# A rebuilt router: logits on unscaled features, a fixed block per expert, token lists by one-hot products

## The chip, the core and the metric

One core of a Trainium2 chip runs one program. The metric is the device time in microseconds (us) of one execution, lower being better; the kernel before is shown by the median of three runs, 2042.06 us (2040.55 to 2044.55). Its profiled execution took 2040.88 us, with a span of 2039.4 us from the first instruction to the last. Times in the tables below are us from the start of the span.

## The reference, cut to what matters

512 tokens of 1024 features pass two layers, an mLSTM and Fourier mixer, and then a mixture of 16 experts in 4 groups. Only its router is changed:

```python
x = x + gate1 * rmsnorm(y, g_post_mix)
h2 = modulate(rmsnorm(x, g_pre_ffn), shift2, scale2)      # h * (1 + scale) + shift
g_logits = h @ w_router_group + b_router_group            # 4 groups
p_group = softmax(g_logits); g_sel = argmax(g_logits)
e_sel = (h @ w_router_expert + b_router_expert)[group g_sel]   # 4 experts
top_v, top_i = top_k(e_sel, 2)
w_top = softmax(top_v) * p_sel
for e in range(16):
    a = silu(h @ w_gate[e]) * (h @ w_up[e])
    y = y + combine[..., e] * (a @ w_down[e])
```

Everything is float32. A token thus goes to two experts; 512 tokens make 1024 pairs.

## The kernel before, in words

Features lie on the partitions, as 8 chunks of 128, and tokens along the columns. Large products are exact to float32 by three passes over high and low parts of the operands (`three_pass`); small ones are plain float32 products on PE. The order on each engine is the order in which the program is written, and every engine waits on counters of the others: `need` adds waits, `do` issues and counts, `join()` makes all engines wait for all. A plain float32 product shows as two rows of the trace, one per pass; a transpose as one.

The projection `w_out_2` (`mix_out`) is streamed by `stream` and `rows_products`: PE multiplies 8 rows of weights into 8 banks, and before its chunk 5 of the first row it runs the last head's transposes (`last_head`, `skip_and_gate`). `rows_root` then forms the root of the mean square, and `Residual.plain` adds the scaled product to X: `chunks` takes the 8 chunks in turn (DVE scales and adds, ACT squares, PE sums the squares over features by four products with a column of ones), `root` takes the root for each token, and `spread` turns it into a row over the columns.

The router (lines 1975 to 2143) then runs step by step:
- 8 multiplications on DVE and 8 additions of the shift on ACT write H2, then `join()`;
- PE forms the logits (32 products and 4 for the bias) and transposes H2 by tokens (32); the 2048 KB of token rows go to HBM (`h2_tokens`);
- DVE chooses a group and two experts by `first_max`, with two visits to ACT for exponentials; PE counts the pairs (`asum`), DVE turns counts into slots. Slots are packed: an expert with n tokens takes ceil(n/128) blocks, one without takes none, and `etab_u` lists the expert of each block;
- POOL scatters the token numbers into a list in HBM (8 indirect DMAs, L2141) and reads the list back (`slot_tokens`);
- `gather(0)` (L2185) fetches the token rows of block 0, `turn_rows` transposes them, `split_rows` splits them.

Weights of a block are 12 units of 512 KB (4 gate, 4 up, 4 down); `fetch` (L2217) issues one on SP's queue, `split_unit` splits one (ACT the high part, DVE the low). The first four of block 0 wait for the table of experts, units 4 and 5 for the scatter, and the others for the first gather. In `block` (L2270) SP fetches the next block's unit as soon as this block's copy is split, PE runs gate, up and down products, and POOL gathers the next block's rows. After the last block, the outputs are gathered by pair and summed.

## Time and profile before

| | us |
|---|---|
| median of three runs | 2042.06 |
| profiled execution | 2040.88 |
| its span | 2039.4 |
| PE busy (share of the span) | 1816.0 (89%) |
| DVE busy | 1217.6 (60%) |
| ACT busy | 917.2 (45%) |
| POOL busy | 112.2 (5%) |

Busy time is summed over the span, and the share hides that the stages differ: the page's 40 slices show PE at 8 or 9 tenths in most, and at 6 in the two from 1580 to 1682 us, which hold most of the router. The granted clock of PE is given as a share of 2.4 GHz: 1.00, or 0.50 for 1.2 GHz. An instruction's row names its output and inputs; "idle before" is how long its engine waited, and for what.

### The profile page before, as it was taken

Reading aid. Unit: us, or ns where it says so; the run is one execution under the profiler, and the core shown is the slowest. Engines: PE = TensorE matmul, PEld = TensorE weight load, DVE = VectorE, ACT = ScalarE, POOL = GpSimd, SP = SyncE. Lnnn points to the kernel's source line nnn. Section 1 sums busy time; section 2 is a strip of 40 time slices with the busy share of each in tenths; the row PEclk is TensorE's granted clock in tenths of the full one; section 3 lists DMA queues with packets and bytes.
Section 4 is the critical chain, followed back from the end, with each engine's and each line's share of the span. In section 5 each row is a group of like instructions: output and inputs, shape, how many; then the busy total and the mean of one; then the engine's idle time right before and its main releaser. Section 6 shows DMA issues by size and latency. Waiting matters only on the chain. (4 is left out here: it accounts for less than half of the span.)

```text
span 2039.4 us, 25515 instructions
## 1 busy us (share of the span) xinstructions
PE 1816.0 (89%) x9142; PEld 1506.0 (74%) x9142; DVE 1217.6 (60%) x2157; ACT 917.2 (45%) x1449; POOL 112.2 (5%) x132
## 2 busy tenths in 40 slices
PE   7897899999998977899999998899877669999993
PEld 6776788888886755778888887785766658888872
DVE  3555668885226556368766324645744358888885
ACT  3446432222224337242223223423833158898984
POOL 1000000000000000001100000100000011011001
PEclk8998899999998989999999997999987679999997
DMA  4323234545322240227544323300120189999993
GB/s 143 90 76 111 72 93 135 145 135 145 103 94 61 64 172 26 76 69 196 165 145 125 102 94 109 85 21 33 53 73 11 47 307 375 372 356 365 353 348 143
DMA packets 206339, 289.88 MB, mean 142 GB/s; under 512 B 14704, under 2 KB 152920, under 8 KB 206120
## 3 DMA queue, kind: packets, MB, share of 16 engines
q1 hardware_dynamic: 188356, 237.98, 35.5%
q0 software_dynamic: 12080, 36.42, 5.8%
q10 hardware_dynamic: 5812, 14.25, 1.9%
q8 instruction: 59, 0.97, 0.2%
q14 instruction: 32, 0.26, 0.0%
HBM read 271.78 MB, written 22.07 MB: 144 GB/s over the span
## 5 line engine op out<-in xcount | busy, mean ns | idle before, releaser
L227 DVE TENSOR_TENSOR weights_low<-ring,weights_high 128x1024 fp32r<-128x1024 f32 x202 | 246.7, 1223 | 407.4 <-ACT weights_high L221 407.3
L200 PE MATMUL bank<-XH,weights_high 128*128 128x512 f32 x1120 | 454.3, 406 | 30.0 <-DVE XL L69 20.3
L202 PE MATMUL bank<-XH,weights_low 128*128 128x512 f32 x1120 | 444.6, 397 | 0.0
L201 PE MATMUL bank<-XL,weights_high 128*128 128x512 f32 x1120 | 443.5, 396 | 0.0
L221 ACT CAST weights_high<-ring 128x1024 fp32r<-128x1024 f32 x202 | 211.1, 1047 | 439.1 <-PE bank L202 438.8
L200 PEld LDWEIGHTS bank<-XH,weights_high 128*128 128x128 f32 x1120 | 215.6, 193 | 78.7 <-ACT squares L69 12.3
L202 PEld LDWEIGHTS bank<-XH,weights_low 128*128 128x128 f32 x1120 | 214.8, 192 | 47.0
L201 PEld LDWEIGHTS bank<-XL,weights_high 128*128 128x128 f32 x1120 | 215.6, 193 | 43.0 <-issue 0.5
L2241 DVE TENSOR_TENSOR XL<-ring,XH 128x1024 fp32r<-128x1024 f32 x144 | 171.2, 1220 | 30.4 <-ACT XH L2235 30.4
L2235 ACT CAST XH<-ring 128x1024 fp32r<-128x1024 f32 x144 | 145.5, 1048 | 0.5 <-PE bank L202 0.3
L69 DVE SCALAR_TENSOR_TENSOR squares<-ring,c_silu,squares 128x128 f32<-128x128 f32 x384 | 135.2, 352 | 13.6
L200 PE MATMUL bank<-hidden_high,weights_high 128*128 128x512 f32 x352 | 137.1, 390 | 0.0
L202 PE MATMUL bank<-hidden_high,weights_low 128*128 128x512 f32 x352 | 137.0, 389 | 0.0
L201 PE MATMUL bank<-hidden_low,weights_high 128*128 128x512 f32 x352 | 136.9, 389 | 0.0
L2241 DVE TENSOR_TENSOR weights_low<-ring,weights_high 128x1024 fp32r<-128x1024 f32 x72 | 86.1, 1218 | 0.1
L189 POOL DMA_DIRECT2D ring<-in_w_ada x48 | 42.4, 884 | 719.9 <-DVE squares L263 719.9
L1111 ACT ACTIVATE tmp<-tmp 128x512 f32<-128x512 f32 x44 | 27.8, 633 | 110.1 <-DVE tmp L1107 110.1
L200 PE MATMUL bank<-weights_high,gathered_high 128*128 128x256 f32 (+1 forms) x216 | 71.4, 331 | 6.2 <-DVE weights_low L2241 5.2
L201 PEld LDWEIGHTS bank<-hidden_low,weights_high 128*128 128x128 f32 x352 | 66.1, 188 | 13.7
L202 PEld LDWEIGHTS bank<-hidden_high,weights_low 128*128 128x128 f32 x352 | 66.1, 188 | 13.7
L200 PEld LDWEIGHTS bank<-hidden_high,weights_high 128*128 128x128 f32 x352 | 66.1, 188 | 13.6
L2235 ACT CAST weights_high<-ring 128x1024 fp32r<-128x1024 f32 x72 | 74.1, 1054 | 0.0
(449 smaller groups left out, 3126.5 us busy)
## 6 DMA issues: line engine op xcount, KB each, us to landing
ring<-in_w_ffn_in SPq DMA_DIRECT2D x88, 512.0 KB, 4.8
ring<-in_w_gate SPq DMA_DIRECT2D x72, 512.0 KB, 5.1
ring<-in_w_up SPq DMA_DIRECT2D x72, 512.0 KB, 7.1
ring<-in_w_down SPq DMA_DIRECT2D x72, 512.0 KB, 5.6
ring<-in_w_ada POOLq DMA_DIRECT2D x48, 512.0 KB, 4.7
ring<-in_w_ffn_out SPq DMA_DIRECT2D x44, 512.0 KB, 3.5
ring<-in_w_out SPq DMA_DIRECT2D x24, 512.0 KB, 3.5
slot_output<-expert_out SPq DMA_DIRECT2D x19, 512.0 KB, 6.7
```

Source lines behind the costliest of these rows:

```text
L69: op(*args, **kw).then_inc(self.line.sem, 1)
L189: queue.eng.dma_start(dst, src).then_inc(ln.sem, 16)
L200: PE.matmul(out_ap, w_h, x_h, start=first, stop=False, skip_group_check=True)
L201: PE.matmul(out_ap, w_h, x_l, start=False, stop=False, skip_group_check=True)
L202: return PE.matmul(out_ap, w_l, x_h, start=False, stop=last, skip_group_check=True)
L221: S.copy(wh[:, s, :], ring[s][:, :]).then_inc(high_done.sem, 1)
L227: V.tensor_tensor(wl[:, s, :], ring[s][:, :], wh[:, s, :].bitcast(F32), ALU.subtract).then_inc(split_done.sem, 1)
L1111: S.activation(sg, sg, ACT.Silu).then_inc(silu_done.sem, 1)
L2235: S.copy(high[s], raw[q]).then_inc(l_high.sem, 1)
L2241: V.tensor_tensor(low[s], raw[q], high[s].bitcast(F32), ALU.subtract).then_inc(l_split.sem, 1)
```

## The change

1. `Residual` gets a router. For each chunk ACT also writes X times the gain (`xg`, unnormalized), and PE multiplies it with the router's weights into bank 1, behind the sums of squares. The root for each token is applied to the logits (`lgm`) and to the token rows (`half_rows`) afterwards; `spread` and H2 are gone. The share of the shift and the bias (`router_row`), the shift as a row (`shift_row`) and a row of column numbers (`iota_row`) are made by 18 products on PE and four copies on ACT ahead of `mix_out`; the router's weights are loaded by POOL's queue before that.
2. Each expert owns block e; only tokens beyond 128 go to further blocks from 16 on. The first 16 entries of the table are constants, and block 0 is expert 0's.
3. Both experts are chosen in all groups at once, the arithmetic of the pair weights comes after `split_rows(0)`, and the exponentials with it.
4. The list of tokens for all blocks comes from eight products of one-hot matrices (`at_place`, `tokens_at`) straight into `idx`; scatter, list in HBM and its load are gone.
5. Eight of block 0's weight units are fetched before the residual chunks, the last four once the token rows are stored, whose tiles they share (`h2t = raw[8:]`). The first four are split before the first gather has landed.

```diff
-                scaled, summed, low, squared = {}, {}, {}, {}
+                scaled, summed, low, squared, routed = {}, {}, {}, {}, {}
...
                     summed[j] = tok
+                    if self.router:
+                        gain, xg, w_router = self.router
+                        pe.need(*bank_free[1], routed[j])
+                        for t in range(TT):
+                            self.logits = pe.do(PE.matmul, bank[1][:, t * 20:(t + 1) * 20],
+                                                xg[:, order[j], t * P:(t + 1) * P], w_router[:, order[j], :],
+                                                start=j + t == 0, stop=False, skip_group_check=True)
...
                     squared[j] = act.do(S.activation, squares[j % 3], X[:, k, :], ACT.Square,
                                         after=[*x_ready[k], *([summed[j - 3]] if j >= 3 else [])])
+                    if self.router:
+                        gain, xg, w_router = self.router
+                        routed[j] = act.do(S.activation, xg[:, k, :], X[:, k, :], ACT.Copy, scale=gain[:, k:k + 1])
...
                 self.root()
-                self.spread()
-                return self.token_root
+                return self.rooted
...
+        load(pool, lr, wrt[:, :, 0:4], I["w_router_group_2"][0].rearrange("(k p) n -> p k n", p=P))
...
+        shift_row = con[:, where["rope_cos"][0]:where["rope_cos"][0] + D]
+        for half in range(2):
+            pe.need(*bank_free[6 + half])
+            for c in range(4):
+                k = 4 * half + c
+                t = pe.do(PE.matmul, bank[6 + half][:, c * P:(c + 1) * P], section(0, SHIFT2)[:, k:k + 1].broadcast_to([P, P]),
+                          ident, start=True, stop=True)
+            shift_ready = act.do(S.copy, shift_row[:, half * 512:(half + 1) * 512], bank[6 + half][:, :],
+                                 after=[t, row_read[6]])
+            bank_free[6 + half] = [shift_ready]
+        pe.need(lr.now(), *bank_free[3])
+        for k in range(KC):
+            pe.do(PE.matmul, bank[3][:, 0:20], section(0, SHIFT2)[:, k:k + 1].broadcast_to([P, P]), wrt[:, k, :],
+                  start=k == 0, stop=False)
+        pe.do(PE.matmul, bank[3][:, 0:20], ones[0:1, :], brow[:, :], start=False, stop=True)
+        t = pe.do(PE.matmul, bank[3][:, P:2 * P], const("token")[:, 0:1].broadcast_to([P, P]), ident, start=True, stop=True)
+        act.do(S.copy, router_row[:, :], bank[3][:, 0:20], after=[t])
+        router_consts = act.do(S.copy, iota_row[:, :], bank[3][:, P:2 * P])
+        bank_free[3] = [router_consts]
         spread = mix_out(I["w_out_2"][0], None, out_order, out_ready, between=last_head)
         m_ctx.close()
-        router_norm = Residual(POST_MIX, spread).plain()
...
-        for k in range(KC):
-            t = vec.do(V.scalar_tensor_tensor, H2[:, k, :], X[:, k, :], PRE_FFN[:, k:k + 1], rstd_t[:, :], ALU.mult,
-                       ALU.mult, after=[router_norm])
-            act.do(S.activation, H2[:, k, :], H2[:, k, :], ACT.Identity, bias=section(0, SHIFT2)[:, k:k + 1], after=[t])
-        join()
-        for t4 in range(TT):
-            for k in range(KC):
-                t = pe.do(PE.matmul, bank[0][:, t4 * 20:t4 * 20 + 20], H2[:, k, t4 * P:(t4 + 1) * P], wrt[:, k, :],
-                          start=k == 0, stop=False, after=[lr.now()])
-            logits = pe.do(PE.matmul, bank[0][:, t4 * 20:t4 * 20 + 20], ones[0:1, :], brow[:, :], start=False, stop=True)
...
-        load(act, lh2, h2d.rearrange("(t p) d -> p t d", p=P), h2t[:, :, :], after=[vec.line.now(), act.line.now()])
...
+        h2t = raw[8:]
...
+        sp.need(split_done.now(), lfill.now())
+        for q in range(UNITS - 4):
+            if q == len(ring):
+                sp.need(vec.line.now(), act.line.now(), pe.line.now(), used_done.now())
+            fetch(0, 0, q, first=True)
+        for q in (act, vec):
+            q.need(vec.line.now(), act.line.now(), pe.line.now(), used_done.now())
+        xg = x_tok[:, :, :].rearrange("p t d -> p (t d)").rearrange("p (k t) -> p k t", k=KC)
+        norm3 = Residual(POST_MIX, spread, router=(PRE_FFN, xg, wrt))
+        token_root = norm3.plain()
+        rstd_c = roots[:, 1, :].unsqueeze(2)
+        def half_turn(i):
+            b = (3, 4, 5, 6, 7, 0)[i % 6]
+            pe.need(*bank_free[b])
...
+                k = 4 * (i % 2) + c
+                t = pe.do(PE.transpose, bank[b][:, c * P:(c + 1) * P], xg[:, k, (i // 2) * P:(i // 2 + 1) * P], ident)
+            half_turned[i] = t
+        def half_rows(i):
+            b, cols = (3, 4, 5, 6, 7, 0)[i % 6], slice((i % 2) * 512, (i % 2 + 1) * 512)
+            t = vec.do(V.scalar_tensor_tensor, h2t[i // 2][:, cols], bank[b][:, :], roots[:, 1, i // 2:i // 2 + 1],
+                       shift_row[:, cols], ALU.mult, ALU.add, after=[half_turned[i], token_root, shift_ready])
+            bank_free[b] = [t]
+            if i % 2:
+                load(sp, lh2, h2d[(i // 2) * P:(i // 2 + 1) * P, :], h2t[i // 2], after=[t])
+        half_turned = {}
+        for i in range(6):
+            half_turn(i)
...
+        vec.do(V.tensor_copy, etab_u[:, 0:NE], iota[:, 0:NE])
+        t = vec.do(V.tensor_tensor, lgm[:, :, :], bank[1][:, 0:TT * 20].rearrange("p (t n) -> p t n", t=TT),
+                   bc(rstd_c, TT, 20), ALU.mult, after=[norm3.logits, token_root, router_consts])
...
+        tm1 = vec.do(V.tensor_reduce, m1[:, :, 0], el[:, :, :], AX, ALU.max, after=[te])
...
+        te = vec.do(V.tensor_tensor, less1[:, :, :], el[:, :, :], bc(m1[:, :, :], TT * 4, 4), ALU.is_lt, after=[tm1])
...
+        te = vec.do(V.scalar_tensor_tensor, less1[:, :, :], less1[:, :, :], 100.0, iota4e, ALU.mult, ALU.add, after=[te])
...
+        te = vec.do(V.tensor_reduce, at1[:, :, 0], less1[:, :, :], AX, ALU.min, after=[te])
...
+        t1 = vec.do(V.tensor_tensor, oh1[:, :, :], iota4e, bc(at1[:, :, :], TT * 4, 4), ALU.is_equal, after=[te])
...
+        t = vec.do(V.tensor_tensor, asum[:, :, :], A[:, 0], A[:, 1], ALU.add, after=[ta, t2])
...
+        pe.need(t, *bank_free[2])
+        ranks, count = bank[2][:, 0:TT * NE], bank[2][:, TT * NE:(TT + 1) * NE]
+        pe.do(PE.matmul, ranks, const("before"), asum[:, :, :].rearrange("p t n -> p (t n)"), start=True, stop=False,
+              skip_group_check=True)
+        for u in range(TT - 1):
+            for v in range(u + 1, TT):
+                t = pe.do(PE.matmul, bank[2][:, v * NE:(v + 1) * NE], ones[:, :], asum[:, u, :], start=False,
+                          stop=u == TT - 2, skip_group_check=True)
+        for u in range(TT):
+            counted = pe.do(PE.matmul, count, ones[:, :], asum[:, u, :], start=u == 0, stop=u == TT - 1,
+                            skip_group_check=True)
+        for i in range(3):
+            half_rows(i)
+        half_turn(6)
+        half_turn(7)
...
+        tr = vec.do(V.tensor_scalar, full1[:, :, :], rank, float(P), None, ALU.is_ge, after=[counted])
...
+        tr2 = vec.do(V.scalar_tensor_tensor, full[:, :, :], rank, float(2 * P), full1[:, :, :], ALU.is_ge, ALU.add, after=[tr])
...
+        tp = vec.do(V.scalar_tensor_tensor, place[:, :, :], full[:, :, :], float(-P), rank, ALU.mult, ALU.add, after=[tr2])
...
+        tc = vec.do(V.tensor_tensor, full1[:, :, :], full1[:, :, :], moved[:, :].unsqueeze(1).broadcast_to([P, TT, NE]),
...
+        tb = vec.do(V.tensor_reduce, blk_j[:, :], a_blk[:, :, :, :].rearrange("p j t n -> p (j t) n"), AX, ALU.add, after=[tb])
+        t = vec.do(V.tensor_tensor, tokens_at[:, :, :], iota[:, 0:BLOCKS].unsqueeze(1).broadcast_to([P, 2 * TT, BLOCKS]),
+                   blk_j[:, :].unsqueeze(2).broadcast_to([P, 2 * TT, BLOCKS]), ALU.is_equal, after=[tb])
...
+        tn = vec.do(V.tensor_tensor, tokens_at[:, :, :].rearrange("p (j t) b -> p j t b", j=2),
+                    tokens_at[:, :, :].rearrange("p (j t) b -> p j t b", j=2),
+                    token_less[:, :].unsqueeze(1).unsqueeze(3).broadcast_to([P, 2, TT, BLOCKS]), ALU.mult, after=[t, tl])
...
+        for i in range(2 * TT):
+            t = vec.do(V.tensor_scalar, at_place[:, i, :], iota_row[:, :], place_j[:, i:i + 1], None, ALU.is_equal)
+            listed = pe.do(PE.matmul, bank[1][:, 0:BLOCKS], at_place[:, i, :], tokens_at[:, i, :], start=i == 0,
+                           stop=i == 2 * TT - 1, after=[t, tn])
+        half_rows(3)
+        half_rows(4)
+        idx_ready = vec.do(V.tensor_scalar, idx[:, :], bank[1][:, 0:BLOCKS], float(T), None, ALU.add, after=[listed])
+        bank_free[1] = [idx_ready]
+        for i in range(5, 8):
+            half_rows(i)
+        cleared = vec.do(V.memset, hg[:, :], 0.0)
...
+        table = vec.do(V.tensor_scalar, etab_u[:, BLOCKS:BLOCKS + 1], inc[:, NE - 1:NE], float(NE - 1), None, ALU.add)
+        empty = vec.do(V.memset, yt[:, :], 0.0)
+        for q in (act, vec):
+            q.need(used_done.now(), split_done.now())
+        for q in range(AHEAD):
+            split_unit(0, q, first=True)
...
+        for q in (pe, act):
+            q.need(*[x for b in range(8) for x in bank_free[b]])
...
+        token_rows()
+        pool.need(idx_ready, cleared, lh2.now())
+        gather(0)
         for q in engines:
             q.need(*[x for b in range(8) for x in bank_free[b]])
-        sp.need(vec.do(V.memset, yt[:, :], 0.0))
-        pool.need(vec.do(V.memset, hg[:, :], 0.0))
...
-        load(pool, l_idx, idx[:, :], idxd.rearrange("(p b) o -> p (b o)", p=P))
-        pool.need(l_idx.now())
-        gather(0)
         turn_rows(0)
         for half in range(2):
             split_rows(0, half)
-        SP.wait_ge(vec.line.sem, table[1])
-        sp.need(lfill.now())
-        e = SP.value_load(etab_u[0:1, 0:1], min_val=0, max_val=NE - 1)
-        for q in range(UNITS):
-            if q == len(ring):
-                sp.need(lh2.now(), vec.line.now(), act.line.now(), pe.line.now(), lsc.now())
-            if q == len(ring) + 2:
-                sp.need((l_hg, 16))
-            fetch(0, e, q, first=True)
-        for q in range(AHEAD):
-            split_unit(0, q, first=True)
+        t = vec.do(V.tensor_tensor, e4[:, :, :], gl[:, :, :], bc(gm[:, :, :], TT, 4), ALU.subtract, after=[tgm])
+        exp1 = act.do(S.activation, e4[:, :, :], e4[:, :, :], ACT.Exp, after=[t])
...
+        t2 = vec.do(V.tensor_reduce, p2[:, :, 0], picked2[:, :, :], AX, ALU.add, after=[t2])
...
+        t = vec.do(V.tensor_tensor, wts[:, 0, :], p1[:, :, 0], psel[:, :, 0], ALU.mult, after=[t, t2])
+        vec.do(V.tensor_tensor, wts[:, 1, :], wts[:, 0, :], p2[:, :, 0], ALU.mult, after=[t])
...
+        r_ctx.close()
+        sp.need(empty, table, lh2.now())
+        for q in range(UNITS - 4, UNITS):
+            fetch(0, 0, q, first=True)
```

On PE, in the chunks of the last residual sum (`xg` is called x_tokens, since it lies in that tile), "-" is before and "+" the change:

```order
-L69 MATMUL bank<-ones,squares 128x1 x8
+L69 MATMUL bank<-ones,squares 128x1 x4
+L69 MATMUL bank<-w_router,x_tokens 128x20 x4
+L69 MATMUL bank<-ones,squares 128x1 x4
+L69 MATMUL bank<-w_router,x_tokens 128x20 x4
 L69 MATMUL bank<-ones,spare 128x1 x4
```

Each group of four sums of squares is now followed by four router products.

On PE, just ahead of the first products of the projection `w_out_2`, after the transposes of the third head:

```order
 L69 MATMUL bank<-state,tmp 128x129
 L69 MATMUL bank<-const_tables,z_and_u 128x128 x4
+L69 MATMUL bank<-const_tables,modulation_biased 128x128 x8
+L69 MATMUL bank<-w_router,modulation_biased 128x20 x8
+L69 MATMUL bank<-b_router,ones 128x20
+L69 MATMUL bank<-const_tables 128x128
 L200 MATMUL bank<-XH,weights_high 128x512
 L201 MATMUL bank<-XL,weights_high 128x512
```

Eighteen small products have come in; nothing has left.

On SP's queue, the last eight units of block 0 before (behind the load of block 0's expert from the table and the four gate units; the names in brackets are counters; slots_scattered counts the scatter, rows_gathered the gather):

```order
L2227 DMA ring<-in_w_up 128x1024 [waits pe_done,act_done,slots_scattered,vec_done,h2_stored]
L2227 DMA ring<-in_w_up 128x1024
L2227 DMA ring<-in_w_up 128x1024 [waits rows_gathered]
L2227 DMA ring<-in_w_up 128x1024
L2227 DMA ring<-in_w_down 128x1024 x4
```

and with the change, from the projection's weights to the loop over blocks:

```order
L189 DMA ring<-in_w_out 128x1024 [waits split_done] x7
L2116 DMA ring<-in_w_gate 128x1024 [waits slot_output_filled,split_done]
L2116 DMA ring<-in_w_gate 128x1024 x3
L2116 DMA ring<-in_w_up 128x1024 [waits pe_done,used_done,act_done,vec_done]
L2116 DMA ring<-in_w_up 128x1024 x3
L189 DMA h_tokens<-ring 128x1024 [waits vec_done] x4
L2116 DMA ring<-in_w_down 128x1024 [waits h2_stored,vec_done]
L2116 DMA ring<-in_w_down 128x1024 x3
```

The waits on the table, the scatter and the gather are gone; the token rows are stored from this queue in four pieces, and only the last four units wait for that.

## Rows read from the trace of the kernel before

**Rows 1.** Windows: the stages; us, busy of PE, PEld, DVE, ACT, POOL, clock, DMA, GB/s

```profile
1550.00:1552.00 2.00, 1.02 (x8) 0.97 (x8) 0.50 (x2) 0.26 (x1) 0.00 (x0) 1.00 0.00 0
1554.64:1571.26 16.62, 13.78 (x64) 13.73 (x64) 11.10 (x17) 5.31 (x10) 0.00 (x0) 0.50 0.00 0
1571.26:1603.25 31.99, 23.32 (x112) 22.50 (x112) 8.13 (x13) 7.94 (x13) 0.00 (x0) 0.55 0.04 3
1603.25:1610.65 7.40, 0.00 (x0) 0.00 (x0) 5.52 (x30) 1.70 (x3) 0.00 (x0) 0.75 0.72 285
1610.65:1616.92 6.27, 6.27 (x29) 6.27 (x30) 0.00 (x1) 0.00 (x0) 0.00 (x0) 0.50 0.01 3
1616.92:1626.13 9.21, 7.17 (x48) 6.93 (x47) 7.40 (x35) 5.19 (x10) 0.00 (x0) 0.80 0.00 0
1626.13:1638.36 12.23, 0.00 (x0) 0.00 (x0) 1.54 (x2) 0.00 (x0) 7.78 (x9) 0.56 0.52 172
1638.36:1652.68 14.32, 1.98 (x8) 1.58 (x8) 2.57 (x4) 3.33 (x5) 3.05 (x5) 0.50 0.57 196
1652.68:1673.89 21.21, 21.17 (x108) 17.89 (x108) 16.87 (x19) 17.63 (x22) 2.10 (x2) 0.87 1.01 387
1673.89:1693.36 19.47, 18.74 (x108) 16.00 (x109) 16.52 (x19) 17.41 (x23) 2.10 (x2) 1.00 0.98 366
```

**Rows 2.** The page's DMA issues: queue, count, KB each, us to landing

```profile
ring<-in_w_gate SPq DMA_DIRECT2D x72, 512.0 KB, 5.1
...
slot_output<-expert_out SPq DMA_DIRECT2D x19, 512.0 KB, 6.7
```

**Rows 3.** Timeline of PE: start, us, instruction, count, idle before and what ended it

```profile
1504.15 1.11 PE L69 MATMUL bank<-const_tables,z_and_u 128*128 128x128 f32 x4 [5.10 <-DVE z_and_u L69]
...
1550.50 1.02 PE L69 MATMUL bank<-ones,tmp 128*128 128x1 f32 x8 [2.84 <-DVE tmp L69]
...
1556.97 3.54 PE L69 MATMUL bank<-ones,squares 128*128 128x1 f32 x16 [2.94 <-DVE tmp L69]
...
1581.21 3.58 PE L69 MATMUL bank<-w_router,h 128*128 128x20 f32 x16 [7.76 <-ACT h L69]
...
1597.48 5.01 PE L69 MATMUL bank<-const_tables,h 128*128 128x128 f32 x32
```

**Rows 4.** Timeline of DVE in the residual sum and the router

```profile
1554.68 0.75 DVE L69 SCALAR_TENSOR_TENSOR tmp<-bank,gains,rstd 128x512 f32<-128x512 f32 x1 [2.65 <-ACT rstd L69]
...
1603.73 0.17 DVE L69 TENSOR_TENSOR r_penalty<-r_logits,r_m 128x16 f32<-128x16 f32 x1
1603.94 0.17 DVE L69 SCALAR_TENSOR_TENSOR r_penalty<-r_penalty,const_tables 128x16 f32<-128x16 f32 x1
...
1610.11 0.23 DVE L69 TENSOR_TENSOR r_pair<-r_group,r_second 128x64 f32<-128x64 f32 x1
1610.37 0.23 DVE L69 TENSOR_TENSOR r_pairs<-r_pair 128x64 f32<-128x64 f32 x1
...
1623.05 0.54 DVE L69 TENSOR_TENSOR r_compare<-r_blocks_to,const_tables 128x368 f32<-128x368 f32 x1
```

**Rows 5.** Timelines of SP, POOL, PE and DVE around the first gather

```profile
1638.21 9.91 SPq L2227 DMA_DIRECT2D ring<-in_w_up  x4
...
1642.03 0.18 POOL L2189 COPY tokens_now<-slot_tokens 128x1 uint32<-128x1 uint32 x1 [3.08 <-DMA slot_tokens<-slot_token]
1643.12 1.07 POOL L2192 DMA_INDIRECT gathered<-h_tokens,tokens_now  x1 [0.91 <-POOL tokens_now L2189]
...
1647.34 1.98 PE L2201 MATMUL bank<-const_tables,gathered 128*128 128x128 f32 x8 [23.24 <-DMA gathered<-h_tokens,tokens_now]
...
1649.97 1.29 DVE L2210 TENSOR_TENSOR gathered_low<-bank,gathered_high 128x512 fp32r<-128x512 f32 x2 [22.14 <-ACT gathered_high L2208]
```

**Rows 6.** DMAs that read h2_tokens (the gathers), and the store that writes it

```profile
DMA to landing us min/median/max: 4.2/6.5/7.5
...
h_tokens<-h_tok ACTq DMA_DIRECT2D x1, 2048.0 KB, 7.0
```

254 lines of the change are left out of this document (113 added, 141 removed).

## The prediction

> **What bounds the kernel now.** I read the page first: the span is 2039.4 us, the profiled execution 2040.88, the median of the runs 2042.06. Then I cut the time around the router into stages, from the moment at 1554.64 when DVE begins the residual sum until the first product of the first expert block at 1652.68. The reader should see in [rows 1] that these seven stages, 98.04 us in all, are one chain that is handed from engine to engine: for most of it one engine works at a time, and what stands behind it can begin only then. From 1652.68 the blocks run, 21.21 us for the first and 19.47 for the next, with PE at 18.74 of 19.47. The DMA share is near 1 there too, but at 387 GB/s in the first block against 366 in the second, so the weights could come faster; PE and its hand-overs set the cadence. So each us that the first product comes earlier is a us off the end, and what follows the blocks is not touched.
>
> The number of blocks must be the same for that. 72 loads of gate weights, 4 per block, make 18 blocks, and 19 output stores fit (one more than blocks) [rows 2]. The new table has 16 blocks plus one for each further 128 tokens of an expert. Worked out from the reference on its inputs, the experts get 20 to 175 tokens, none gets none, and two get over 128 (175 and 138): 18 blocks, as before.
>
> **The change, part by part.** "Gain" is against the profiled execution.
>
> Products beside the chunks. The name promises cover, but in that stage PE is the slow engine: 13.78 of 16.62 us busy from 1556.97 on, while DVE has 11.10 and ACT 5.31 [rows 1, 3]. The sums of squares are 32 float32 products with one column each, and 8 of them take 3.54 us at the clock of 0.50 (1.2 GHz). The router's 32 products have 20 columns and take 3.58 for 8, since it is the 128x128 operand that costs [rows 3]. They go in line: 13.78 + 4 x 3.58 = 28.1, so the logits are there at 1585.0 and the stage lasts 30.4 in place of 16.62. The eight added ACT instructions fit (about 0.6 each, like the eight squares and two others in its 5.31), ACT having 11 us free.
> The Trainium skill, "TensorE: Matmul & The Clock Gate", Part 1, says that activity releases the clock; by that rule the doubled run of products would be at 2.4 GHz. In this trace a PE that is busy without a break from 1556.97 stays at 0.50, so I follow the row.
>
> Root on the sums. The spread of the root, the eight H2 multiplications and additions, the products at 1581.21 and the transposes: 31.99 us [rows 1], all removed from the path. The new transposes (24) follow the products on PE under DVE's arithmetic.
>
> Choice of experts. A step between dependent DVE instructions is 0.21 for 16 columns and 0.26 for 64 [rows 4]. The change has 6 narrow and 16 wide ones: 1.3 + 4.2 = 5.4, and no visit to ACT, against 7.40. Then 11 products in place of 14: at 0.50 they cost 6.27/14 = 0.45 each, 4.9; at 1550.50, with the clock at 1.00, a float32 product is 1.02/4 = 0.26 (the row counts two passes for each), 2.8 [rows 1, 3]. The transposes before it brought the clock up in this trace (32 in 5.01, 0.16 each, where two passes cost 0.44 [rows 3]), so I take 3.3.
>
> Places and token lists. 7 narrow and 7 of 64 columns, 3.3; six of 128 or 184 columns, between 0.26 and the 0.54 of 368 columns [rows 4], I take 0.32, 1.9; eight one-hots of 128 columns at 0.28, 2.2; five half rows at 0.75 [rows 4], 3.8; the list 0.2. Together 11.4, against 9.21. The eight list products hide under one-hots and half rows.
>
> The scatter, 12.23 [rows 1], is gone, and so is the load of the list behind it (1638.36 to 1642.03, 3.7 [rows 5]). In its place stands a wait for the last quarter of h2, which is stored only after the last half row: before, the 2048 KB store was out of the way early. A store takes 7.0 us for 2048 KB, and 6.7 for 512 KB when the DMA is full [rows 2, 6]; this one meets an idle DMA. Bounds 3 and 7, I take 3.9, near the first gather's 4.2, which also met little traffic.
>
> First gather and first product. Index copy to gather 1.09; landing 4.2 at best and 6.5 as median [rows 5, 6]. The four loads of down weights leave on the same signal as this gather, so I take 5.5. From the landing to the end of the split rows is 1647.34 to 1651.26, 3.9 [rows 5]; the 1.4 that PE then waited for weights falls away, as four units are split beforehand.
> The Trainium skill, "DMA: Bandwidth & Descriptors", section on queues, rings and completion order, says that an engine goes round its queues packet by packet. By that the gather shares with the loads rather than waiting behind them; this trace's median of 6.5 under full load agrees.
>
> Sum: 30.4 + 5.4 + 3.3 + 11.4 + 3.9 + 1.1 + 5.5 + 3.9 = 64.9 in place of 98.04: gain 33.1.
>
> First block. It took 21.21 - 19.47 = 1.74 more than the next at a mean clock of 0.87 [rows 1]. Now PE transposes tokens until just before; I take half of it back, 0.9. The pair weights' arithmetic, now ahead of the loop on DVE and ACT (some 14 steps of 0.21 and a table load), lies under the 24 gate products, whose weights are ready; uncovered it would cost 1 to 2.
>
> Before the out projection PE gets 18 float32 products: 4.6 at full clock, 8.1 at half. They meet a pause of 5.10, in which PE waits for DVE until 1504.15 [rows 3]. Bounds: 4.6 - 5.10, and a little below since PE comes out of the pause at a higher clock, -1; and 8.1 - 5.10, +3. I take +0.5. Of the ACT copies there (four, under 0.6 each) the last two wait for these products, and the scaling that DVE needs at 1505.3 is queued behind them: same bounds.
>
> The early loads of eight weight units meet idle DMA and cost nothing; if they did not exist, the first block would wait for them. The router's loads, moved to POOL's queue, have no wait ahead of them on that queue and the mLSTM heads to land in.
>
> Net gain 33.1 + 0.9 - 0.5 = 33.5: 2007.4 against the profiled 2040.88, and **2008.5** against the median 2042.06, which is 1.2 above it.
>
> **The rivals.**
> 1. Late transfers: the last store takes 7 and the gather 7.5, its worst [rows 6]; PE's new work ahead of the projection costs 3, the small products run at half clock (+1.6), and the first block stalls 2 for its fifth unit. Against it: DMA is idle when the store starts. Singly these are inside the range; most of them together: 2042.06 - 33.5 + 10 = 2018.
> 2. The clock rises in the chunk stage. The 64 products cost 0.26 each, 16.6, hardly more than today's stage, and 11.5 more is gained: 1997. It is what the rule of the Trainium skill quoted above would give. Against it speak 13.78 us of unbroken work at 0.50, and the 20-column products, whose 0.45 each is the same price.
> 3. Blocks are added, and the kernel is slower. Every expert without tokens costs a block of 19.47 [rows 1] that the packed table skipped. The sum turns at 33.5 / 19.47 = 1.7 empty experts: with two, 2042.06 - 33.5 + 38.9 = 2047.5. The trace alone allows one (15 experts and 3 further blocks make 18 too), two as well; the counts worked out above speak against.
> 4. The weights' stream, not PE, sets the blocks. Then the first product's date does not count but the date from which the DMA is full. Before, that was about 1648 [rows 5], with six units of the first block still to come; now it is about 1609, with four. At 1.4 us per unit the gain would be 39 + 3 less a break of some 4 while block 1 waits for buffers: about 38, 2004. It is inside the range.
>
> **How the numbers follow.** Forecast (with rival 4) 0.78, rival 1 0.12, rival 2 0.07, rival 3 0.02, and 0.01 for no change, if some wait that I do not see holds the first block where it is. The favourable bounds (gather at 4.2, front -1, full clock in the small products, 0.9 in block 0) give 4.2 less than 2008.5, rival 4 the same, and some slack on the DVE steps 2 more: 2002. The unfavourable ones, of which a few meet, reach 2016, which takes in most of rival 1 but not 2 and 3. About 0.2% is what a measurement of this kernel can tell from no change: faster 0.97, same 0.01, slower 0.02.
>
> **What would show it.** The first gate product near 1619; the chunk stage about 28 us of unbroken PE at 0.50, with logits near 1585; a DVE chain of 5 to 6 us, then small products of 3 to 5; the gather issued near 1611; blocks still 19.47 apart, 18 of them. The prediction is wrong if the stage of the chunks is under 20 us (clock), if the first gather leaves after 1616 (store or DVE), if the residual sum begins over 3 us later than 1554.64, or if there are not 72 gate loads.

## The result, and the profile after

The change took the kernel from a median of 2041.68 us to 2012.65 (2012.3 to 2017.94), a ratio of 0.9862 with a 95% interval of 0.9843 to 0.9881: faster by 1.4%, 29.0 us. The forecast was 2008.5, the range 2002 to 2016. The profiled execution took 2012.73 us, its span 2011.3; PE is busy for 1821.5 us (91%), DVE 1213.3, ACT 915.3, POOL 108.5.

Single executions of one kernel, the kernel before among them, can differ by 5 to 6 us. In the traces that have such a surplus it is there before 45 us: PE's clock rises to 1.00 at 24 us in the trace of the changed kernel, and only at 37 us in its second trace, in a stretch that no version touches. So the traces are compared from a fixed instruction on, which stands behind that stretch and is called the mark: the transposes of the third mLSTM head, at 1492.84 in the kernel before and at 1493.84 after. The first gate product of block 0 stands 159.84 us behind it before (1652.68) and 129.94 after (1623.78): 29.9 us gained there. Block 0 adds 0.2, and the two ends take 2.0 back: the mark itself is 1.0 late, 0.9 of it before 27 us, and the end is 1.0 late behind block 1, where two of the last output gathers on POOL took 1.28 and 1.71 us and the other six 0.95. That makes the 28.1 between the spans.

First the stages, as in [rows 1]: windows of the changed kernel (us; busy of PE, PEld, DVE, ACT, POOL; clock, DMA share, GB/s). They are the residual sum with the chunks, the choice of experts, ranks and counts, places and lists with half rows, the last store and the list copy, the first gather, its turn and split, block 0, block 1.

```profile
1559.38:1589.26 29.88, 27.50 (x129) 27.53 (x130) 11.16 (x18) 11.67 (x19) 0.00 (x0) 0.50 0.19 71
1589.26:1593.13 3.87, 3.87 (x19) 3.87 (x19) 3.63 (x23) 2.30 (x3) 0.00 (x0) 0.50 0.01 2
1593.13:1596.81 3.68, 3.68 (x31) 3.68 (x30) 1.98 (x3) 0.00 (x0) 0.00 (x0) 0.85 0.37 146
1596.81:1606.66 9.85, 4.49 (x24) 4.13 (x22) 8.59 (x34) 0.00 (x0) 0.00 (x0) 0.54 0.18 74
1606.66:1611.57 4.91, 4.77 (x23) 4.80 (x24) 4.52 (x8) 1.30 (x3) 1.15 (x1) 0.52 0.62 218
1611.57:1619.47 7.90, 2.92 (x27) 2.71 (x26) 2.40 (x3) 3.89 (x8) 1.08 (x1) 0.92 1.01 385
1619.47:1623.78 4.31, 1.95 (x8) 1.56 (x9) 1.52 (x6) 2.22 (x3) 1.22 (x2) 0.50 0.99 362
1623.78:1644.76 20.98, 20.86 (x109) 17.67 (x109) 15.07 (x28) 16.68 (x23) 2.09 (x2) 0.89 0.57 195
1644.76:1664.23 19.47, 18.81 (x109) 16.13 (x109) 16.51 (x19) 17.41 (x23) 2.09 (x2) 1.00 0.97 360
```

The first seven make 64.4 us where 98.04 stood, against a forecast of 64.9. So the sum was met within 0.5, with luck: its terms are off by 3.6 one way and by 3.2 the other. Most of the missing 4 us lie ahead of it.

The timeline of PE, against [rows 3]: the front, the chunk stage, the small products.

```profile
1493.84 1.06 PE L69 MATMUL bank<-const_tables,z_and_u 128*128 128x128 f32 x4
1494.69 2.23 PE L69 MATMUL bank<-const_tables,modulation_biased 128*128 128x128 f32 x16
1496.76 1.86 PE L69 MATMUL bank<-w_router,modulation_biased 128*128 128x20 f32 x16
...
1504.54 0.80 PE L200 MATMUL bank<-XH,weights_high 128*128 128x512 f32 x1 [4.47 <-ACT iota_row L69]
...
1510.80 0.60 PE L69 MATMUL bank<-const_tables,z_and_u 128*128 128x128 f32 x4
...
1561.76 1.84 PE L69 MATMUL bank<-ones,squares 128*128 128x1 f32 x8 [3.08 <-ACT squares L69]
1563.46 1.87 PE L69 MATMUL bank<-w_router,x_tokens 128*128 128x20 f32 x8
...
1589.06 5.35 PE L69 MATMUL bank<-const_tables,x_tokens 128*128 128x128 f32 x24
...
1594.41 2.36 PE L69 MATMUL bank<-r_pairs_sum,ones 128*128 128x16 f32 x20
```

The 18 new products take 4.4 us at a granted clock of 0.93, as bounded. Then PE stands for 4.47 us in the output projection, because of an ACT instruction, and the last head's transposes come at 1510.80 in place of 1504.15. The chunk stage is what was forecast: PE without a break from 1561.76 to 1589.06, sums at 1.84 and router products at 1.87 for four.

The timelines of DVE, then POOL, SP and PE, in the router and around the first gather, against [rows 4, 5]:

```profile
1559.38 0.75 DVE L69 SCALAR_TENSOR_TENSOR tmp<-bank,gains,rstd 128x512 f32<-128x512 f32 x1 [2.90 <-ACT rstd L69]
...
1589.26 0.24 DVE L69 TENSOR_TENSOR r_logits<-bank,roots 128x80 f32<-128x80 f32 x1 [1.20 <-PE bank L69]
...
1590.05 0.22 DVE L69 TENSOR_TENSOR r_first_less<-r_expert_logits,r_first_max 128x64 f32<-128x64 f32 x1
1590.19 0.17 DVE L69 TENSOR_TENSOR r_group_less<-r_group_logits,r_group_max 128x16 f32<-128x16 f32 x1
...
1592.64 0.22 DVE L69 TENSOR_TENSOR r_pairs<-r_second,r_group 128x64 f32<-128x64 f32 x1
1592.90 0.23 DVE L69 TENSOR_TENSOR r_pairs_sum<-r_pairs 128x64 f32<-128x64 f32 x1
...
1596.81 0.22 DVE L69 TENSOR_SCALAR r_past_first<-bank 128x64 f32<-128x64 f32 x1 [1.71 <-PE bank L69]
...
1604.50 0.18 DVE L69 TENSOR_SCALAR slot_tokens<-bank 128x23 uint32<-128x23 f32 x1 [1.01 <-PE bank L69]
```

```profile
1609.46 1.15 POOL L2078 COPY tokens_now<-slot_tokens 128x1 uint32<-128x1 uint32 x1 [320.99 <-DMA h_tokens<-ring]
1611.57 1.08 POOL L2081 DMA_INDIRECT gathered<-h_tokens,tokens_now  x1 [0.96 <-ACT gain_row L69]
```

```profile
1609.52 1.76 SPq L2116 DMA_DIRECT2D ring<-in_w_down  x4
1613.27 2.12 SPq L2116 DMA_DIRECT2D ring<-in_w_gate  x4
1615.73 0.38 SPq L2343 DMA_DIRECT2D slot_output<-expert_out  x1
```

```profile
1619.47 1.95 PE L2090 MATMUL bank<-const_tables,gathered 128*128 128x128 f32 x8 [4.98 <-DMA gathered<-h_tokens,tokens_now]
1623.78 0.79 PE L200 MATMUL bank<-weights_high,gathered_high 128*128 128x512 f32 x1 [2.35 <-DVE gathered_low L2099]
```

The residual sum begins at 1559.38 (1554.64 before). The choice of experts begins as two chains of DVE instructions laid into each other, 0.14 us from row to row (1590.05, 1590.19), where instructions that need each other's result step by 0.26 (1592.64, 1592.90). The gather is issued at 1611.57 and has landed when PE turns the rows at 1619.47. Two things have not moved: 72 gate loads and 19 output stores again, and 19.47 us per block.

### The profile page after: what moved, and what is told of

Read it like the earlier page. It is cut to its first block and busy times, and to the rows that moved or that the text cites. A ratio compares the mean times of both kernels' runs of the same rounds, so it can differ in the third digit from the quotient of the medians.

```text
span 2011.3 us, 25551 instructions
## 1 busy us (share of the span) xinstructions
PE 1821.5 (91%) x9172; PEld 1512.9 (75%) x9172; DVE 1213.3 (60%) x2158; ACT 915.3 (46%) x1448; POOL 108.5 (5%) x127
```

## The experiments

Each run's time is a median of its executions, with its ratio to the kernel before on the same chip; the ratio is formed from all executions and is not the quotient of two medians. Square brackets hold its 95% interval. "Counted" means from the mark of the same trace. The changed kernel itself came first.

> The changed kernel itself, as the yardstick of the others on the same chip: 2012.6 us, with its runs within 0.3%, and the first gate product 28.9 us earlier than in the kernel before. If the 0.96 us by which its trace lies behind the one of before already at 500 us belongs to one execution (the first loads, before 30 us), it has another size here; if it belonged to the change it would be 0.96 again.

2017.86 us (2013.18 to 2018.81), ratio 0.9864 [0.9844, 0.9884]; its trace has the late rise of the clock in the opening, so the ratio and the counted times are the yardstick. Counted, the gather is issued after 117.8 us and the first gate product comes after 130.0 (129.94 in the other trace). Told by its place in the order of DVE's instructions, the row at 502.90 of the changed kernel's first trace (501.98 before) is at 509.20 here, 6.3 later, of which 5.3 arise between 27 and 45 us: from 28 to 37 us PE's granted clock is 0.50 here and 1.00 in the first trace. In the front's trace below, whose program is the same up to the pause, it is at 501.87. So the late mark belongs to single executions and not to the change.

**The front.** The block of 18 products and four copies goes to where PE waits for DVE before the last head's outputs, into banks 0, 2 and 3.

```diff
+            if n == 2 * MH + 1:
+                for half in range(2):
+                    pe.need(*bank_free[2 * half])
...
+                router_consts = act.do(S.copy, iota_row[:, :], bank[3][:, P:2 * P])
+                bank_free[3] = [router_consts]
             if 2 <= n < 2 * MH + 2:
                 outputs(n - 2)
...
-        for half in range(2):
-            pe.need(*bank_free[6 + half])
...
-        bank_free[3] = [router_consts]
         spread = mix_out(I["w_out_2"][0], None, out_order, out_ready, between=last_head)
```

> Only the place of the 18 router products and their four ACT copies is changed: into the pause of PE before the last head's outputs, into banks 0, 2 and 3. Theory A (the copies are queued on ACT behind the last head's root, and the output projection's second chunk waits for bank 3 until then): the projection runs through its first seven chunks by about 1502, the last head's transposes stand at about 1505 instead of 1510.80, the residual sum begins at 1555.5 to 1556.5 instead of 1559.38, and the kernel takes 3 to 4 us less than the changed one, 2009 us. Theory B (what is lost is the 4.4 us of the 18 products themselves, wherever they stand): the projection begins no later, but the last head's outputs do, by up to 4 us, and the time stays within 1 us of the changed kernel's. Theory C (the clock of PE after the pause is what costs): the transposes come at 1505 and yet the sum begins after 1558.

2009.41 us (2006.9 to 2014.65), ratio 0.9839 [0.9822, 0.9856]. PE and ACT in that run:

```profile
1485.29 1.95 PE L69 MATMUL bank<-const_tables,modulation_biased 128*128 128x128 f32 x16
1487.47 1.93 PE L69 MATMUL bank<-w_router,modulation_biased 128*128 128x20 f32 x16 [0.23 <-DVE mlstm_small L69]
...
1489.98 0.39 PE L69 MATMUL bank<-v_tokens,ring 128*128 128x129 f32 x2
...
1503.93 0.70 PE L69 MATMUL bank<-const_tables,z_and_u 128*128 128x128 f32 x4 [4.85 <-DVE z_and_u L69]
```

```profile
1492.73 1.05 ACT L69 COPY const_tables<-bank 128x512 f32<-128x512 f32 x2
...
1493.75 0.25 ACT L69 COPY iota_row<-bank 128x128 f32<-128x128 f32 x1
...
1501.83 0.29 ACT L69 ACTIVATE mlstm_stats<-mlstm_stats,epsilon 128x4 f32<-128x4 f32 x1
```

The products fit into the pause (1485.29 to 1489.98), and the copies are done at 1494, long before the last head's root at 1501.83 (its row on ACT). The transposes come 11.24 us after the mark (16.96 in the changed kernel), the residual sum begins after 61.42 (65.54 in the changed kernel, 61.8 in the kernel before), and the first gate product comes 4.1 earlier. Theory A holds, and B and C fall: the same 18 products cost nothing here. Banks 6 and 7 were exchanged for 0 and 2 in the same edit; that PE waited for bank 3 is read from the row at 1504.54, which names the copy of `iota_row`. What cost was the order on ACT: the last copy, which frees bank 3, was queued behind the last head's root, and PE, whose second chunk needs bank 3, stood in front of it with six of its first seven chunks still to do.

**The gather.** The down units of block 0, and all that SP fetches behind them, wait for it.

```diff
-        sp.need(empty, table, lh2.now())
+        sp.need(empty, table, lh2.now(), (l_hg, 16))
```

> Only this is changed: the four down units of the first block (and with them all later fetches of SP) wait for the first gather's landing. Theory A (the gather is slow because it shares the DMA with four down units, four gate units and a store): it lands 4 to 5 us after its issue instead of 7.9, the first gate product comes about 3 us earlier, near 1621, and the time falls by as much, to 2009.5, since the down units are needed only 11 us later. Theory B (7.9 us is what this gather costs on an idle DMA too, since it is issued late or its descriptors are slow): no change in the landing. Theory C (the delayed weights are missed later): the gather lands early but the first block takes 23 us or more instead of 20.98, and nothing is gained.

2009.53 us (2007.03 to 2012.71), ratio 0.9829 [0.9813, 0.9846]. The gather lands 4.3 us after its issue where 7.7 stood, by the DMA view:

```profile
gathered<-h_tokens,tokens_now POOLq DMA_INDIRECT x1, 7.7
```

```profile
gathered<-h_tokens,tokens_now POOLq DMA_INDIRECT x1, 4.3
```

```profile
1621.01 1.20 PE L2090 MATMUL bank<-const_tables,gathered 128*128 128x128 f32 x8 [1.62 <-DMA gathered<-h_tokens,tokens_now]
1624.56 0.79 PE L200 MATMUL bank<-weights_high,gathered_high 128*128 128x512 f32 x1 [2.35 <-DVE gathered_low L2099]
```

Theory A holds. The turn takes 1.20 in place of 1.95 besides (PE had waited for 1.62 us only, not 4.98), so the first gate product comes 4.0 earlier. The later down units are not missed: from the first gate product to the second block's hidden rows it takes 32.8 us (32.6). The Trainium skill, "DMA: Bandwidth & Descriptors", section on queues, rings and completion order, has the engines go round their queues by packets; the traces agree in that the gather lands 7.7 us after its issue with SP's loads beside it and 4.3 without them, and yet ahead of a gate unit that left at 1615 and took 8.8 us.

**The half rows.** 3 and 4 stand before the ranks are read.

```diff
-        for i in range(3):
+        for i in range(5):
             half_rows(i)
...
-        half_rows(3)
-        half_rows(4)
+        half_rows(5)
+        half_rows(6)
```

> Only the order on DVE is changed: half rows 3 and 4 stand before the rank counts are read, in the 1.71 us in which DVE waits for them, and 5 and 6 behind the one-hots. Theory A (the date of the last half row, and with it of the last store, decides over the gather): the last half row ends 1.4 us earlier, the store lands 1.4 earlier, the gather and the first product too, and the kernel takes 1.4 us less than the changed one. Theory B (the list of tokens or something else behind it holds the gather): the half row is earlier, the gather is not.

2011.42 us (2009.42 to 2017.18), ratio 0.9838 [0.9823, 0.9853]. The gather is issued 1.3 us earlier (counted 116.5), and lands after 8.7 us, so that the first gate product gains 0.3. Theory A is right up to the gather, and the result is neither theory's: beside the same loads most of the gain is lost again. The front's run had seen the same, 5.1 earlier at the gather and 4.1 behind it.

**Late loads.** The eight early units of block 0 are fetched behind the table.

```diff
-        for q in range(UNITS - 4):
-            if q == len(ring):
-                sp.need(vec.line.now(), act.line.now(), pe.line.now(), used_done.now())
-            fetch(0, 0, q, first=True)
...
+        sp.need(table, vec.line.now(), act.line.now(), pe.line.now(), used_done.now())
+        for q in range(UNITS - 4):
+            fetch(0, 0, q, first=True)
```

> Undoes the part of the change that fetches the first block's gate and up units ahead of the router: all twelve are issued once the table is ready, behind the last half row. Theory A, the prediction's (the early loads meet an idle DMA and without them the first block would wait): eight more units of 512 KB stand before or beside the first gather, the first gate product comes 3 to 8 us later than in the changed kernel (at the trace's 1.4 us per unit, 8 units are 11 us, of which some 5 lie under the gather that is awaited anyway), and the first block is no shorter: 2016 to 2021 where the changed kernel has 2012.6. Theory B (the gather's wait covers them all): within 1 us of it.

2017.25 us (2016.37 to 2022.12), ratio 0.988 [0.9861, 0.9898]. The first gate product comes 134.6 after the mark, 4.6 later. The gather lands after 7.7 again, at 1618.3; PE turns its rows only at 1624.02, released by ACT's x_tokens copies (1619.90 to 1623.92), which are queued behind the splits of the late units:

```profile
1624.02 1.95 PE L2090 MATMUL bank<-const_tables,gathered 128*128 128x128 f32 x8 [0.77 <-ACT x_tokens L69]
```

So the early loads are worth 4.6 us, as theory A had it, though their place of action is ACT's queue and not the gather.

**Double products.** Each router product is issued twice.

> Every router product beside the chunks is issued twice, the second time into unused columns of the same bank. Theory A (in line at the low clock): 32 products at 0.45 us add 14.3 us to the chunk stage, 29.9 becomes 44, and the granted clock stays at 0.50 through more than 40 us of unbroken work. Theory B (PE's work lies beside the chunks or more activity raises the clock): the stage grows by less than 8 us.

2027.08 us (2024.37 to 2032.44), ratio 0.9929 [0.991, 0.9947]. The windows of the unbroken stretch, in the changed kernel, then in this one:

```profile
1561.76:1589.06 27.30, 27.30 (x128) 27.30 (x129) 8.85 (x15) 10.69 (x18) 0.00 (x0) 0.50 0.16 63
```

```profile
1558.93:1599.88 40.95, 40.95 (x192) 40.95 (x193) 8.86 (x15) 12.40 (x20) 0.00 (x0) 0.50 0.11 43
```

13.65 us more for 32 products, 0.43 each, and 41 us of a fully busy PE at 0.50. Theory A holds.

**The three edits together.**

> The three edits of the first experiments together: the constants' products in the earlier pause, half rows 3 and 4 before the ranks, the down units held until the first gather has landed. Counted from the transposes of the third head the first gate product stood at 129.94 us in the changed kernel; the edits alone brought 4.1, 0.3 (with the gather issued 1.3 earlier, but landing after 8.9 instead of 7.9) and 4.0. Theory A (the gather's landing is set by its neighbours on the DMA, so that the earlier issue counts fully once they are held): 4.1 + 1.3 + 4.0 = 9.4 earlier, 120.5, and about 2003. Theory B (the gains overlap, as the first and third both end at the gather's landing): 7 to 8 earlier, 2005.

2001.53 us (2000.78 to 2003.78), ratio 0.9797 [0.9784, 0.9811]. The first gate product comes 119.75 after the mark, 10.2 earlier; the gather, issued 6.0 earlier, lands after 4.2. 6.0 at the issue, 3.5 in the landing and 0.7 in the turn make it up. Theory A holds, and beats its own sum of 9.4 by 0.8, since the 4.1 of the front had already lost 1.0 in the gather.

**Operands exchanged.** The next question was whether the clock could be had in the chunk stage.

```diff
-                        for t in range(TT):
-                            self.logits = pe.do(PE.matmul, bank[1][:, t * 20:(t + 1) * 20],
-                                                xg[:, order[j], t * P:(t + 1) * P], w_router[:, order[j], :],
-                                                start=j + t == 0, stop=False, skip_group_check=True)
+                        self.logits = pe.do(PE.matmul, bank[1][0:20, :], w_router[:, order[j], :], xg[:, order[j], :],
+                                            start=j == 0, stop=j == KC - 1)
```

> The router products with their operands exchanged: the 128x20 weights are held and 512 columns of the scaled chunk move past, one product per chunk instead of four, with one ACT copy and four small transposes behind them. Theory A (what the stage costs is the exchange of 128x128 operands at the low clock, and a float32 product of 512 columns takes 1.45 to 1.7 at the low clock and 0.9 to 1.0 at the high one, by rows of the mLSTM stage): if the clock stays at 0.50 the stage is 0 to 3 us shorter and 2 are paid behind it, about the same time. Theory B (few columns per product are what keeps the clock down): the granted clock rises to 1.0 within the stage, the sums become cheaper too (0.24 each instead of 0.44), the stage takes 17 to 20 us instead of 29.9, and the kernel 2001 to 2005.

2019.41 us (2014.33 to 2023.69), ratio 0.9874 [0.9852, 0.9896]. Theory B falls: one product of 512 columns takes 1.82, four of 20 took 1.71, and the clock stays at 0.50. Theory A has the clock, but not the time: counted, the first gate product comes after 135.5 us, 5.6 later than in the changed kernel. 2.9 of that are there at the logits, and the last store of h2 landed after 4.9 us in this trace where it took 2.6.

```profile
1567.00:1596.00 29.00, 28.84 (x80) 15.37 (x80) 9.02 (x15) 9.59 (x17) 0.00 (x0) 0.50 0.16 62
```

**Squares added on DVE.** On top of the three edits; DVE is free for most of the stage, and `rows_root` does it so already.

```diff
+                        if j:
+                            summed[j] = vec.do(V.tensor_tensor, square_sum[:, :], square_sum[:, :], squares[j % 3], ALU.add,
+                                               after=[squared[j], summed[j - 1]])
...
+                    for t in range(TT):
+                        summed[KC - 1] = pe.do(PE.matmul, bank[2][:, t:t + 1], square_sum[:, t * P:(t + 1) * P],
+                                               ones[:, 0:1], start=t == 0, stop=t == TT - 1, skip_group_check=True)
```

> On top of the three edits together (2001.5 us, first gate product 119.8 us after the third head's transposes): the squares of the eight chunks are added up on DVE, as the projection's root already does it, and PE takes the sum over features once, with 4 products in place of 32. PE loses 28 products of 0.44 us, 12.4 us; DVE gains 7 additions of 0.68, so that its chunk (scale, add, add) takes 2.05 and the stage is DVE's: some 16.5, and 4 to 5 behind it for the last chunk's square, its router products and the four sums. Theory A (PE's line of small products at the low clock is what the stage takes): 21 to 22 us from the residual sum to the logits instead of 29.9, and 1993 to 1995. Theory B (something else holds the chunks, or DVE's work is in the way): 26 or more, above 1998.

1993.41 us (1992.81 to 1999.62), ratio 0.9761 [0.9744, 0.9778].

```profile
1559.16 13.81 PE L69 MATMUL bank<-w_router,x_tokens 128*128 128x20 f32 x64 [3.70 <-DVE X L69]
1572.80 1.85 PE L69 MATMUL bank<-ones,square_sum 128*128 128x1 f32 x8
```

```profile
1556.17:1575.26 19.09, 16.10 (x76) 16.13 (x77) 14.99 (x25) 10.51 (x18) 0.00 (x0) 0.50 0.30 111
```

The stage is 19.1 us where 29.9 stood, better than theory A's 21 to 22, which had put the last chunk's square and products wholly behind DVE; they overlap. The first gate product comes 110.85 after the mark, 8.9 earlier.

**Wide products.** On top of the three edits, sums with 128x128 ones held, router with 128x96 held (20 columns and zeros), 512 columns moved in both.

```diff
+                        tok = pe.do(PE.matmul, bank[2][:, :], ones[:, :], squares[j % 3], start=j == 0, stop=j == KC - 1)
...
+                        self.logits = pe.do(PE.matmul, bank[1][0:96, :], w_router[:, order[j], :], xg[:, order[j], :],
```

> On top of the three edits together: all products beside the chunks are made large. The sums hold the 128x128 ones and move 512 columns of squares, the router holds 128x96 (its 20 columns and zeros) and moves 512 columns; two products per chunk in place of eight, then two copies and eight small products. The exchange of both operands alone, with 20 columns held and one-column sums between, left the clock at 0.50 for 29 us. Theory A (a PE that works through wide operands is granted 1.00, as the discrete transform's 512-column float32 products before 1418 are): after a few us each product takes 0.95 instead of 1.82, the stage 16 to 20 us, and the kernel is 8 to 11 us faster than with the three edits. Theory B (the clock does not depend on the shape here): 0.50 throughout, 29 us and 2 behind it, the kernel 1 to 3 us slower than with the three edits.

1996.31 us (1994.44 to 1999.05), ratio 0.9766 [0.9751, 0.9781]. PE in the stage:

```profile
1563.66 2.05 PE L69 MATMUL bank<-squares,ones 128*128 128x512 f32 x2 [3.08 <-ACT squares L69]
...
1567.20 1.91 PE L69 MATMUL bank<-squares,ones 128*128 128x512 f32 x2
1568.91 1.21 PE L69 MATMUL bank<-x_tokens,w_router 128*96 128x512 f32 x2
1569.96 1.02 PE L69 MATMUL bank<-spare,ones 128*128 128x512 f32 x2
```

```profile
1567.00:1582.00 15.00, 14.40 (x37) 6.10 (x35) 6.26 (x11) 6.74 (x12) 0.00 (x0) 0.92 0.07 29
```

At 1569 the clock rises to 1.00 and the products go from 1.91 to 1.02. The stage is 21.4 us with the copies and small products behind it, 19.1 without; counted, the first gate product comes at 111.47, 8.3 before that of the three edits. The medians, from two chips, differ by 5.2. Theory A holds in its mechanism and at the lower end of its gain, as the first 5 us are still at the low clock and 2.3 are paid behind (1580.35 to 1582.67).

**Both.** DVE adds the squares, and the router product is wide.

> The squares added on DVE and, beside them, the router's product as 128x96 held and 512 columns moved, one per chunk. PE then has 8 products of 0.95 to 1.9 us in a stage of 16. Theory A (the stage is DVE's, whatever PE's clock is): logits 80.5 us after the third head's transposes minus 0 to 1.5, since the last chunk's products cost 1 to 2 us with the copy and the small transposes, where four 20-column products and the sums cost 3.6; 1992 to 1994. Theory B (a PE that is half idle between wide products gets no higher clock): the granted clock stays at 0.50, the last product takes 1.85, and the time is that of the version with the additions alone or 1 us more. Theory C (the wide products raise the clock even with pauses): 1.00 in the second half of the stage, and the transposes of the tokens that follow take 0.12 each from the start instead of 0.19.

1989.9 us (1989.16 to 1995.7), ratio 0.9747 [0.9732, 0.9763]: the best version, 52 us faster than the kernel before and 23 than the changed one.

```profile
1558.41 7.42 PE L69 MATMUL bank<-x_tokens,w_router 128*96 128x512 f32 x10 [3.70 <-DVE X L69]
1566.60 1.10 PE L69 MATMUL bank<-x_tokens,w_router 128*96 128x512 f32 x2 [0.76 <-ACT x_tokens L69]
...
1573.37 4.50 PE L69 MATMUL bank<-const_tables,x_tokens 128*128 128x128 f32 x24
```

```profile
1555.40:1573.47 18.07, 11.86 (x29) 4.34 (x30) 14.99 (x25) 11.18 (x19) 0.00 (x0) 0.77 0.32 116
```

The logits come 79.5 after the mark, 1.0 to 1.5 sooner than with the additions alone: theory A. B falls, and C is half right: the granted clock is 1.00 from 1564 to 1571 although PE waits 0.77 before each of the last three products of 1.10 us, but it falls again, and the 24 transposes behind them take 4.50, 0.19 each, at a mean of 0.61.

To compare on one chip, the version with the additions alone ran once more beside this one.

> The version with the additions alone once more, on the chip of the one beside it: 1993.4 us, first gate product 110.9 us after the third head's transposes, as before.

1992.68 us (1992.1 to 1998.66), ratio 0.9762 [0.9746, 0.9778], counted 111.35. The version with both is faster than it by 2.8 us in the medians of the same chip and 3.2 counted. 1.5 of that are there at the logits; the rest stems from the last store of h2, which lands after 4.4 and 4.5 us in the two traces of the additions alone, after 4.9 in the one with the operands exchanged, and after 2.6 in the others. Why stays open.

## Why the prediction was right, and where it missed

Counted to the end of block 0, 30.1 us were gained where the prediction's terms say 33.5. The forecast lay in its range, and the mechanism of the largest terms was right; the misses are the front and the gather, and some terms came out by luck. By its own steps, forecast and measured:

| step | forecast | measured | effect on the gain |
|---|---|---|---|
| front: 18 products, four copies | 0.5 | 3.7 | -3.2 |
| residual sum to logits | 30.4 | 29.9 | +0.5 |
| choice of experts | 5.4 | 3.9 | +1.5 |
| rank and count products | 3.3 | 3.7 | -0.4 |
| places, lists, half rows | 11.4 | 9.85 | +1.5 |
| last store, list copy | 3.9 + 1.1 | 4.9 | +0.1 |
| landing of the gather | 5.5 | 7.9 | -2.4 |
| turn and split to first product | 3.9 | 4.3 | -0.4 |
| gained in block 0 | 0.9 | 0.2 | -0.7 |

**What bounds the kernel** was read rightly: seven stages in one chain, then PE at 19.47 per block. The first gate product's 29.9 us came through whole, and rival 4 (the stream of weights as the bound) has nothing for it: in every version the end stands 386.3 to 387.6 us behind the first gate product (386.7 before), also where the down units and all loads behind them were held back. There are 18 blocks, so rival 3 is out too.

**The chunk stage** is the step that decided most, and it was right in mechanism and size: the 64 products go in line at the low clock (the doubled ones show it), and rival 2, the clock that rises by itself, is refuted for products of this shape.

**The front** is the step that failed. "They meet a pause of 5.10", with bounds of -1 and +3, counted PE's time, which was right, and named what is queued behind ACT's copies. It did not ask what stands ahead of the copies on ACT, nor which banks PE needs next. Nor was the pause empty from its start: PE enters it with seven chunks done, and the wait for bank 3 let six of them slip behind it, to be done from 1504.54 on, the first 4 us at a clock of 0.50, and ahead of the last head's transposes. 3.7 us in place of 0.5, outside the bounds, and it broke the text's own condition, a residual sum more than 3 us late (3.7 counted). The run with the block elsewhere gives all of it back.

**The gather**: the prediction saw the four down units beside it and took 5.5 between 4.2 and 7.5. It took 7.7 by the DMA view, above every gather of the kernel before, as not only the down units but block 1's four gate units and an output store were in flight too. The term was mis-sized; with the neighbours held it is 4.2 to 4.4. Which of the neighbours costs what was not separated.

**The last store and the list copy** came out right by luck. From the last half row to the start of the copy it took 2.8 where 3.9 stood, and from the copy to the gather's issue 2.1 where 1.1 stood, as the copy took 1.15 us and not 0.18 (last section).

**Two DVE terms** were too high by 1.5 each. They counted a full step per instruction, but the code interleaves chains that don't need each other, and those step by 0.12 to 0.14; the eight one-hots took 1.65 us together where 2.2 stood. The list products did not hide wholly (1.01 us of waiting at 1604.50), and the rank products waited 1.1 for the 24 transposes that stand ahead of them on PE; both are inside the measured terms.

**Block 0** gave 0.2 of its 0.9: PE had waited 4.98 and 2.35 us for gather and split, and began at the low clock again. The arithmetic of the pair weights cost nothing there, as said.

Rival 1 (late transfers and front together, 2018) came true by half: the front's 3 and the gather's 2, but neither a store of 7, nor small products at half clock, nor a stall in block 0.

## What to carry to other kernels

Work put into a pause is free only if nothing behind it in the same queue waits for what it holds: for each tile or bank that the moved work writes, ask who frees it, and what stands ahead of that instruction on its engine. A single small transfer on the critical path, such as this gather, is worth issuing alone (7.7 against 4.3 us); bulk loads that are needed ten microseconds later can wait for it. And where many small products run in line, first let another engine add up what they add (the first gate product came 8.9 us earlier here), or give PE few wide ones (8.3).

## What was unexpected of the hardware

Being busy did not raise PE's clock: 27.3 us, and with doubled products 41 us, of float32 products without a pause ran at 0.50 (1.2 GHz), with 1 or 20 columns moved against a 128x128 operand, and so did 29 us in which half of the time went to 512 columns moved against 20 held. With 512 columns moved against 96 or 128 held PE had worked for some 5 us when the clock rose to 1.00 (2.4 GHz), and it stayed there between them even with waits of 0.77 us. The Trainium skill, "TensorE: Matmul & The Clock Gate", Part 1, says that activity releases the clock; these traces differ from it, as 27.3 and 41 us of unbroken work went by at 0.50. What makes the difference was not separated. Nor is it the same in every execution: in the opening of one and the same program the clock rose at 24 us in one trace and at 37 in the other.

POOL's first copy of a token list, 128x1 numbers, took 1.13 to 1.20 us in ten of the traces, 0.37 and 0.48 in the two with the squares on DVE alone, and 0.18 with the late loads, as all later copies do; beside none of those does DVE run a subtraction. In the changed kernel it runs from 1609.46 to 1610.61, and DVE's first subtraction of 128x1024 from 1609.41 for 1.2 us; in the version with the additions it ends at 1595.95, and DVE's pair of subtractions (from 1593.61, 2.29 us) at 1595.90. In all twelve traces in which a subtraction runs beside the copy, the copy ends 0.04 us behind it; so it seems to wait until DVE's running instruction ends. The Trainium skill, "GPSIMD Engine Reference", section 8, has the two engines in contention where a DVE instruction reads two inputs from SBUF, as these do; the traces agree, and the late loads, which take the subtraction away, take the delay away too (0.18), though no run was made for it alone.
